# Transposing the scaled outputs of the mixer's first two branches one step later

## The reference

```python
o_a = diff_attention(aq, ak, av, lam, lam_init, subln_g, rel_bias[:, :A_HEADS])
o_b = dilated_attention(bq, bk, bv, rel_bias[:, A_HEADS:A_HEADS + B_HEADS])
o_c = dsa_attention(cq, ck, cv, iq, ik, iw, rel_bias[:, A_HEADS + B_HEADS:])
o = jnp.concatenate([o_a, o_b, o_c], axis=-1)
return o @ w_out
```

```python
attn = p[:, :, 0] - lam * p[:, :, 1]
...
return rmsnorm(o, subln_g) * (1.0 - lam_init)
```

## Time and profile before

| | |
|---|---|
| median of 3 runs | 3626.06 us (3623.41 to 3627.65) |
| profiled execution | 3623.92 us, span 3622.1 us |
| TensorE busy | 3446.2 us (95%) |
| VectorE, ScalarE, GpSimd busy | 1569.8 us (43%), 1007.4 us (28%), 73.5 us (2%) |
| mean granted clock of TensorE | 0.98 |
| mixer steps 0 to 33 | 1764.2 to 2074.2 us of the span |

### The profile page before, as it was taken

One profiled execution on the slowest core, in us unless ns is written; L12 is line 12 of the kernel. 1 busy time (PEld: TensorE's weight loads), 2 busy tenths in 40 slices (PEclk: granted clock), 3 DMA queues, 4 the chain that ended last, 5 costly groups with the idle time before them and its releaser, 6 DMA issues.

```text
span 3622.1 us, 31111 instructions
## 1 busy us (share of the span) xinstructions
PE 3446.2 (95%) x12370; PEld 1816.9 (50%) x12370; DVE 1569.8 (43%) x2824; ACT 1007.4 (28%) x2125; POOL 73.5 (2%) x91
## 2 busy tenths in 40 slices
PE   7999999999999999999999999899889999999998
PEld 3556555555456445444566455664444444444443
DVE  2056191144056351542343463654345555253433
ACT  4244112002244011122688745531111000000001
POOL 0000000020000000100000000000000000000000
PEclk9999999999999999999999999899999999999999
DMA  5100121131000101111101002111001101111111
GB/s 206 56 6 13 57 87 61 53 108 38 26 7 13 34 32 47 41 45 40 41 24 36 27 21 70 48 46 48 24 18 40 47 35 45 42 42 42 40 41 64
DMA packets 49903, 163.72 MB, mean 45 GB/s; under 512 B 5296, under 2 KB 8624, under 8 KB 49085
## 3 DMA queue, kind: packets, MB, share of 16 engines
q1 hardware_dynamic: 44890, 145.82, 11.6%
q10 hardware_dynamic: 4868, 15.91, 1.3%
HBM read 157.46 MB, written 11.32 MB: 47 GB/s over the span
## 4 chain that ended last, share of the span: by engine, by line
PE 85%; DVE 7%; ACT 6%; issue 1%; SPq 1%; DMA 0%; POOL 0%; DVEq 0%; ACTq 0%; POOLq 0%
PE ps L520 34%; PE ps L1189 14%; PE ps L549 8%; PE ps L961 5%; PE ps L677 4%; PE ps L972 2%; ACT sb L1725 2%; PE ps L700 2%; PE ps L856 2%; PE ps L689 2%; PE ps L984 1%; PE ps L1039 1%; PE ps L1050 1%; PE ps L1138 1%; DVE sb L1998 1%
## 5 line engine op out<-in xcount | busy, mean ns | idle before, releaser
L520 PE MATMUL ps<-sb 128*128 128x512 f32 (+1 forms) x3088 | 1241.0, 563 | 14.0 <-ACT sb L1528 6.7
L520 PEld LDWEIGHTS ps<-sb 128*128 128x128 f32 x3088 | 589.1, 191 | 659.7 <-issue 634.8
L1248 ACT ACTIVATE sb<-ps 128x512 f32<-128x512 f32 (+10 forms) x709 | 350.4, 510 | 1516.9 <-PE ps L520 467.0
L1189 PE MATMUL ps<-sb 128*128 128x512 f32 x1232 | 531.6, 594 | 2.8 <-DVE sb L2604 2.8
L1189 PEld LDWEIGHTS ps<-sb 128*128 128x128 f32 x1232 | 234.5, 190 | 299.3 <-issue 293.9
L549 PE MATMUL ps<-sb 128*128 128x512 f32 x672 | 291.5, 594 | 2.4 <-ACT sb L1248 1.9
L961 PE MATMUL ps<-sb 128*128 128x512 f32 x512 | 232.5, 602 | 0.0
L549 PEld LDWEIGHTS ps<-sb 128*128 128x128 f32 x672 | 127.3, 190 | 163.5 <-issue 156.7
L1725 ACT ACTIVATE sb<-sb 128x384 int8<-128x384 f32 (+2 forms) x192 | 184.4, 962 | 1.0 <-DVE sb L2267 0.5
L1290 ACT ACTIVATE sb<-sb 128x512 f32<-128x512 f32 x128 | 74.6, 610 | 365.9 <-DVE sb L2551 122.5
L2134 DVE SCALAR_TENSOR_TENSOR sb<-sb 128x1310 f32<-128x1310 f32 (+1 forms) x120 | 161.7, 1426 | 0.0
(11 more groups left out here) (245 smaller groups left out, 3105.2 us busy)
## 6 DMA issues: line engine op xcount, KB each, us to landing
sb<-in_w_in SPq DMA_DIRECT2D x73, 512.0 KB, 3.3
sb<-in_w_ada SPq DMA_DIRECT2D x48, 512.0 KB, 4.4
sb<-in_w_up SPq DMA_DIRECT2D x44, 512.0 KB, 3.3
sb<-in_w_down SPq DMA_DIRECT2D x24, 384.0 KB, 3.0
sb<-in_w_out SPq DMA_DIRECT2D x16, 512.0 KB, 3.7
sb<-in_w_mkv SPq DMA_DIRECT2D x16, 512.0 KB, 3.3
rows_dram<-vec_dram ACTq DMA_DIRECT2D x1, 6906.0 KB
sb<-rows_dram ACTq DMA_DIRECT2D x6, 1024.0 KB, 5.5
```

The source lines that it names most:

```text
L520: ins = mm(ps[:, 0:tn], w[:, k, :], src(k, t0, tn), start=(k == 0), stop=(k == nk - 1))
L1189: ins = mm(ps[:, 0:512], stationary(k), moving(k), start=(first and k == 0), stop=(k == 3), skip_group_check=not first)
L1248: return act(out, in_, func, scale=scale)
```

## The change

The pair of outputs of steps n - 3 and n - 2 was transposed in the odd step n; now it is transposed one step later, in the even step that follows. The same holds for ScalarE's scaled copy of it. The places within the step stay the same: ahead of `values2` on TensorE, ahead of `head_root` on ScalarE. There are 16 such pairs, in steps 3, 5, ... 33 before, in steps 4, 6, ... 34 after.

```diff
--- before.py
+++ after.py
@@ -1091,8 +1091,8 @@
                 turn2(n - 1, 1)
             for piece in FILLERS.get((n, 1), ()):
                 fill(*piece)
-            if n >= 2 and n % 2 == 1 and n - 2 < 32:
-                back2(n - 2)
+            if n >= 4 and n % 2 == 0 and n - 3 < 32:
+                back2(n - 3)
             if n >= 1:
                 values2(n - 1)
         def second_half(k, t0, tn):
@@ -1745,8 +1745,8 @@
             count_signs("high", n, (6, 7))
             for piece in FILLERS.get((n, 1), ()):
                 filled(*piece)
-            if n >= 2 and n % 2 == 1 and n - 2 < 32:
-                back(n - 2)
+            if n >= 4 and n % 2 == 0 and n - 3 < 32:
+                back(n - 3)
             if 1 <= n <= 32:
                 head_root(n - 1)
             elif n > 32:
```

## The result

| | before | after |
|---|---|---|
| median of 11 runs each, on one chip | 3624.36 us (3620.60 to 3627.97) | 3633.02 us (3630.37 to 3635.18) |
| ratio to before | | 1.0023, 95% interval 1.0015 to 1.0031 |
| profiled execution | 3623.92 us, span 3622.1 us | 3630.37 us, span 3628.5 us |
| mean granted clock of TensorE in it | 0.98 | 0.98 |

The change costs 8.7 us, 0.24%, in this measurement. The forecast was 4.7 us, and its rival on the slower side, two more falls of the clock, 8.3 us. The first measurement lies at the rival's figure, the second a little under the forecast's.

A forecast was written before the change was run, and what follows sets the result against it. TensorE, busy 95% of the span, was taken as the bound. Shifts from bank waits, 0.22 us of transposes and 0.36 us of copy summed to +4.66 us on 3626.06, about 3630.7 us; range 3625.5 to 3637.

The forecast's parts named there:

- its rival on the slower side: Steps 5 to 27: new waits, longest 2.2 us in step 19, bring two more clock falls; 8.3 us slower; chance 0.20.
- L1077 had no wait to remove: The moved pair of transposes on TensorE does not wait for the division, so moving it removes no wait.
- The banks: First transposes of odd steps 5 to 33 wait for the moved copy's PSUM bank: about 12 waits, 16 to 20 us together.
- the five with a forecast of their own: Odd steps 5, 7, 19, 21 and 23: waits for the copy of 1.5, 1.0, 2.2, 1.2 and 1.0 us.
- ScalarE's cost, the small terms: In pairs of steps with two transpose groups, the copy ahead of `head_root` costs 0.36 us, TensorE regains 0.22: +0.14 us each.
- Behind step 34 nothing absorbs a shift: After the last moved step TensorE leads the other engines again, so the whole +4.66 us stays in the time.
- The sum: Shifts added step by step over steps 5 to 34: +4.66 us on the time.
- the 0.22 us of step 32: Steps 32 to 34 have no bank wait; the +0.22 us of step 32 stays, 33 and 34 cancel.
- The clock: TensorE's existing clock falls in steps 25 to 31, costing 3.5, 1.8 and 1.7 us, were taken to stay.
- The rule on cycling banks: Applied to all the new waits: some four more clock falls, 11.9 us slower, 3638 us; no chance of its own.
- The banks don't matter: Rival: the copy ends in time at the end of even steps, leaving 0 to +1.1 us, 3626.6 us; chance 0.11.
- Faster, by the clock: Rival: in steps 25 to 31 no clock fall is left, 7.0 us come back: -2.3 us, 3623.8 us; chance 0.07.

The follow-up runs named there:

- two later: The pair transposed and copied two steps later than in the kernel before, again in odd steps: 3623.41 us against 3624.88 for before, ratio 0.9997.
- copy behind: The changed kernel with ScalarE's copy placed behind `head_root` and `output` instead of ahead of them: 3641.54 us against 3624.88 for before, ratio 1.0048.
- keep one: The changed kernel, but the one pair of step 18 stays in step 17: 3629.06 us against 3625.84 for before, ratio 1.0011.
- other bank: The changed kernel with the pair transposed into a bank of the fillers' pool, outside the shared rotation: 3629.54 us against 3626.00 for before, ratio 1.0009.
- after, second time: The changed kernel measured again without any edit, the second measurement: 3628.92 us against 3624.88 for before, ratio 1.0012.
- wide only: Against the kernel before, only pairs with t of 4 or more (steps 9 to 15, 25 to 31) moved: 3629.45 us against 3625.84, ratio 1.0015.

## Why the prediction was right, point by point

**L1077 had no wait to remove.** Right: it appears in no list of waits before or after; its view after shows only "issue", 5.3 us in 20 places, where before it had 4.6 us and 0.7 us behind ScalarE's counts.

**The banks.** Right, and in each step by itself. The waits came in twelve odd steps, in the five with a forecast of their own each at its length, and made 19.3 us in all, in the range of 16 to 20. Four runs show the cause: with the old parity they go (two later); with the copy 0.9 us later in the same step they grow by 0.9 us (copy behind); for one pair alone one goes (keep one); with the pair in another bank the transposes wait for the copy no more, and fillers do so for 2.3 us (other bank). That the price is set by ScalarE's full even step is shown by the copy on VectorE, which takes back the whole loss with the rotation left as it is (but for the last pair, in step 33).

**ScalarE's cost, the small terms.** +0.14 us in steps 9 to 15 was forecast four times; measured from step 8 to 16 is 2.13 - 1.56 = 0.57 us, so 0.14 each. "Behind step 34 nothing absorbs a shift": right.

**The sum.** 4.66 us against 4.3 without the new fall. The 0.3 us arose in steps 26 to 31, for which I added 0.28 us (4.16 to 4.44) and the trace shows none (5.76 to 5.79); the 0.22 us of step 32 stayed, as forecast (5.79 to 6.01). No run looks at steps 26 to 31 by themselves.

**The clock.** Here the forecast and its rival share the result. I held the clock's falls to stay as they were, and gave 0.20 to the case of more of them, with step 19's 2.2 us wait as the first to go. It did go, in both traces of the changed kernel: +1.7 us, and with it the start of step 34's scores moved by 5.8 us and not by 4 to 5. Two falls were wanted for that rival to decide. The first trace shows one, and the falls between 1957 and 2062 us, for which the text's bound was a change of more than one, are those of before. In the second trace they are three again, but one is twice as long: estimated as in the prediction, steps 19 to 31 lose 7.0 us to the clock before, 8.5 us in the first trace of after and 10.4 us in the second, which is two falls more.

That the time of the first measurement, +8.7 us, stands inside the range is in part luck. It is nearly twice the forecast and past the 0.2% above which the forecast gave 0.19, and the range reached so far only because it was left open to three falls more.

The medians can be split roughly the same way. Each run lists its mean clock, in thousandths. Time less (1 - clock) x span, the mean over the runs, is 3549.8 to 3550.1 us for before in the first two batches, 3553.5 us for after and 3553.8 us for after, second time. That is 3.4 to 4.0 us that the clock does not explain by this estimate, beside the 4.3 us of the trace. What is left of the 8.7 us lies in the clock: by the same estimate a mean of about 75 us is lost to it in an execution of before (in those batches; for the first measurement its clocks are not listed), 79.6 us in the first measurement of after, 75.5 in the second. Step 19 gives 1.7 us of that where it falls. The rest need not lie in the changed steps: the profiled execution of the second measurement took 3635.06 us, 11.1 us over that of before, of which 3.0 us had come before step 0 and 1.5 us came behind step 34. Where it sits in executions that were not profiled stays open, and with it why the second measurement's runs show none of it in the mean. So does whether +4 or +9 us would come out of a third.

**The rule on cycling banks.** The Trainium skill's rule on cycling through PSUM banks (TensorE: Matmul & The Clock Gate, "A second HAM failure mode: psum-queue depth-cycling"), that it can idle TensorE so often that its clock swings, was weighed in the prediction. Of the waits that the bank rotation made here, those up to 1.5 us left the clock at 1.00 over steps 0 to 18; the one of 2.2 us brought it down in two traces of three. So the danger is real in one step; applied to all the new waits, the prediction made 11.9 us of it, which neither measurement shows.

**The rivals that fell.** "The banks don't matter" is out by the waits. "Faster, by the clock" is out: both traces of after still have three falls in steps 25 to 31, in the second not all in the same steps, and the idle sum of the four odd steps is 13.6 us in the first, against 13.7.

## What to carry to other kernels

When an operation that takes its turn in a small rotation of banks is moved, count the takes through: the wait is not at the operation but at whoever takes its bank next, and one step of shift can put it in front of the engine that bounds the kernel while two steps of shift cost nothing. Before moving work "later", look which engine is late in the new place; a copy of 0.46 us behind a full queue made waits of up to 2.2 us in new places. If the place is wanted, give the copy to the engine that has slack there (here VectorE, at 43% busy): move and copy together gained 0.1% where the bare move lost 0.1 to 0.2%. And a single trace does not settle differences of a few microseconds that hang on the clock: run it twice.

## What was not expected of the hardware

The same step with the same wait does not always meet the same clock: with 2.21 us of idle time before L1050 in step 19, the granted clock of the step was 0.86 in two traces and 1.00 in a third (wide only), where TensorE's work in the step differed only by two transposes and the step began about 2 to 4 us earlier. Step 27, with about 3.3 us of idle time before and 3.4 us after, kept 1.00 in before and in the first trace of after; with the same waits it had 0.89 in two later and in the second trace of after. The fall in step 19 costs 1.7 us, more than the 1.4 us by which the wait itself grew.

VectorE's scaled copy out of PSUM, 128 x 256 in float32, took 0.48 us, and ScalarE's 0.46 us: the place in the queue made the difference, not the engine's speed.
